# A depthwise convolution of 31 taps: its fourth channel block made by GpSimd in a chain of its own

## The chip, the core and the metric

The kernel runs on one core of a Trainium2 chip. The metric is the device time of one execution in microseconds; the kernel before has a median of 2791.62 us over three runs (2791.62 to 2791.8 us).

## What is computed

Two transformer blocks run one after the other on 256 tokens of width 1024 (and on 256 context tokens in the first layer). The part that matters here is the mixer of the first layer, which joins a gated depthwise convolution with an mLSTM. Its convolution branch, cut to what matters:

```python
def _dwconv(x, w, b):                       # w is 31 taps x 512 channels
    pad = (k - 1) // 2
    y = lax.conv_general_dilated(x, w[:, None, :], (1,), [(pad, k - 1 - pad)], ..., feature_group_count=ch)
    return y + b

def merge(p, h_seq):
    a, g, _, _, _, o, _, _ = p              # projections of the normed input
    u = _dwconv(a * jax.nn.sigmoid(g), conv_w, conv_b)
    u = jax.nn.silu(_layer_norm(u, ln_g, ln_b))
    ...
    return jnp.concatenate([u, hm], axis=-1) @ w_out
```

`merge` is done for the 256 context tokens and the 256 latent tokens, so the convolution works on two segments of 256 tokens, 512 columns in all. All of it is float32.

## The kernel before

Channels lie on the 128 partitions, tokens along the free axis. The 512 channels of the convolution are four blocks of 128. `u0[:, b]` is the gated input of block b with 15 zeros on either side of each segment, `u[:, b]` its output, 128 x 512. The weights of the whole network come from memory as a stream of 1 MB slots through a ring of three slots. SyncE loads a slot into the ring as soon as `slot_read` says that the slot three before it has been used.

The mixer, `mixer0`, has two stretches.

**The projections** (about 60 to 184 us of the span). TensorE works through 20 units of weights, each as three products of a leading and a remaining part. ScalarE cuts the leading part of a unit (`Cut.lead`, line 255), VectorE subtracts it to get the rest (`Cut.rest`, line 264), and there are two buffers, so unit g is cut when unit g-2 has been multiplied. Two units share a slot, and the rest of the odd unit frees it. After each even unit from the third on, TensorE does two products of a second stream, the modulation weights (`later_product`, line 396). After the two units of block b VectorE multiplies value and gate into `u0[:, b]` (line 875) and signals `conv_in_ready`.

**The scans** (184 to 274 us). Eight steps i, four heads by two directions. In each, TensorE makes three modulation products, a row (line 690), waits for `m_weights_ready` and `m_h_taken`, and multiplies decay weights by values (line 713); every second step it also makes the scores (line 680). VectorE adds the mask (line 937), multiplies decays by scores (line 950), and normalizes the result (lines 964 to 977).

The convolution fills VectorE's time in both. `taps(n)` issues the next n taps, each one `scalar_tensor_tensor` of 128 x 512 (line 866; the first tap of a block is line 862), always for the block that has the fewest so far; between two taps of the same block it waits for the earlier. The calls are placed by hand: 4 after each `Cut.rest` while the blocks are made (24 taps), 6 or 3 after each later `Cut.rest` (45), 6 at the end of the projections, and `each` at two places of each scan step, which is the number that is left, 49, divided over 13 places and rounded up: 4. When all is done VectorE signals `conv_done` (line 980), and TensorE takes the mean over the channels with all four blocks of `u` (line 722), which it can't start before step 7 is done.

GpSimd in this stage does four memsets (lines 835 to 838) and then nothing until 1129 us. Its instruction order is its own; it waits only on semaphores.

Of the kernel before, what the change touches and what calls it, by code (L numbers as in the profile page):

```python
# [25 lines left out]
T = 256  # L26
TT = T // P
NTOK = 2 * T
CONV, TAPS = 512, 31
PAD = (TAPS - 1) // 2  # L30
HEADS_M, QK_M, V_M = 4, 64, 128
# [74 lines left out]
def program(nc, stream, table, x_in, out, upto=None):  # L106
    ctx_sems = {}

    def sem(name):

        if name not in ctx_sems:
            ctx_sems[name] = nc.alloc_semaphore(name)
        return ctx_sems[name]
# [3 lines left out]
    h = nc.alloc_sbuf_tensor("h", [P, KD, NTOK], F32)  # L117
# [12 lines left out]
    def col(name):  # L130
        a, n = COL[name]
        if a >= NRES:
            return arena[:, ARENA - NTAB + a:ARENA - NTAB + a + n]
        return tab[:, a:a + n]
# [11 lines left out]
    table_ready, x_ready = sem("table_ready"), sem("x_ready")  # L146
# [436 lines left out]
    def mixer0():  # L583
# [4 lines left out]
        u0 = u0.rearrange("p (b s t) -> p b s t", b=4, s=2)  # L588
        u = u.rearrange("p (b t) -> p b t", b=4)
# [11 lines left out]
        small = nc.alloc_sbuf_tensor("m_small", [P, 64], F32)  # L601
# [12 lines left out]
        def tensor(pe):  # L614
            eng = pe.eng
# [102 lines left out]

            eng.wait_ge(sem("m_h_taken"), 2 * HEADS_M)
            eng.wait_ge(sem("conv_done"), 1)  # L720
            for b in range(4):
                mm = nc.tensor.matmul(ps[:, 7, :], col("over512"), u[:, b, :], start=(b == 0), stop=(b == 3))
            mm.then_inc(N["mean"], 1)
# [108 lines left out]
        def gpsimd(pool):  # L832
# [4 lines left out]
            nc.gpsimd.memset(v1[:, :, :, V_M:V_M + 1], 1.0)  # L837
            nc.gpsimd.memset(zero, 0.0).then_inc(sem("m_borders_ready"), 1)

        def vector(dve):  # L840
            eng = dve.eng
            for k in range(KD):
# [5 lines left out]
            eng.wait_ge(sem("m_borders_ready"), 1)  # L848
            eng.wait_ge(sem("table_ready"), 16)
            cw = col("conv_w").rearrange("p (b t) -> p b t", b=4)  # L850
            last, made = [0] * 4, [0] * 4

            def taps(n, ready=4):

                for _ in range(min(n, 4 * TAPS - sum(made))):
                    b = min(range(ready), key=lambda b: made[b])
                    t = made[b]
                    made[b] += 1
                    o = u[:, b, :].rearrange("p (s t) -> p s t", s=2)
                    i = u0[:, b, :, t:t + T]  # L860
                    if t == 0:
                        last[b] = dve.add(nc.vector.tensor_scalar(o, i, cw[:, b, 0:1], col("conv_b")[:, b:b + 1],
                                                                  ALU.mult, ALU.add))
                    else:
                        dve.settle(last[b])
                        last[b] = dve.add(nc.vector.scalar_tensor_tensor(o, i, cw[:, b, t:t + 1], o,
                                                                         ALU.mult, ALU.add))

            for b in range(4):
                for c in range(2):  # L870
                    C.rest(dve, 2 * b + C.buffers + c)
                    if b:
                        taps(4, b)
                eng.wait_ge(sem("conv_gate_ready"), b + 1)
                nc.vector.tensor_tensor(u0[:, b, :, PAD:PAD + T],
                                        ps[:, 2 * (b % 2), :].rearrange("p (s t) -> p s t", s=2),
                                        sg[:, b, :].rearrange("p (s t) -> p s t", s=2), ALU.mult)\
                  .then_inc(sem("conv_in_ready"), 1)
                eng.wait_ge(sem("conv_in_ready"), b + 1)
# [44 lines left out]
            for g in range(8 + C.buffers, 20):  # L924
                C.rest(dve, g)
                piece = pieces.pop(0) if pieces else None
                if piece:
                    piece()
                taps(3 if piece else 6)
            taps(6)  # L930
            each = -(-(4 * TAPS - sum(made)) // (4 * HEADS_M - 3))

            def diagonal(i):

# [7 lines left out]
            for i in range(2 * HEADS_M):  # L942
# [5 lines left out]
                for j in range(4):  # L948
                    for a, b in spans[d][j]:
                        ins = nc.vector.tensor_tensor(dec[:, j, a * P:b * P], dec[:, j, a * P:b * P],  # L950
                                                      ps[:, j, a * P:b * P], ALU.mult)
# [9 lines left out]
                o = ps[:, 5:7, :].rearrange("p a (b c) -> p (a b) c", b=2)  # L961
# [15 lines left out]
                    nc.vector.tensor_tensor(hs[:, :, hd, :], hs[:, :, hd, :], tmp4[:, :, hd, :], ALU.add)\  # L977
                      .then_inc(sem("m_head_ready"), 1)
            dve.settle()
            nc.vector.tensor_copy(small[:, 60:61], u[:, 3, 0:1]).then_inc(sem("conv_done"), 1)  # L980
            eng.wait_ge(sem("mods0_ready"), 2)
            eng.wait_ge(sem("mods1_ready"), 2)
            eng.wait_ge(sem("m_rms_ready"), 1)
# [20 lines left out]
            for hd in range(HEADS_M):  # L1004
                cuts["ab_out"].input_rest(dve, hd, h[:, hd, :])

        return dict(name=name, tensor=tensor, scalar=scalar, vector=vector, gpsimd=gpsimd)


# [1766 lines left out]

    add(start(), ada_first(norms["mix0_mod"]["pe"], norms["mix0_mod"]["act"], norm0.pop("vector")))
    add(norm0, mixer0())
    add(out_proj("mix0_out", "ab_out", 0, mixer0_ready, 0, 2, then="ffn0_mod", nxt="ffn0_up"))
    add(modulate("ffn0_mod", 0, 0, 3, done("mix0_out", "x"), 6, "ffn0_up", held=17))  # L2780
# [18 lines left out]
    if upto is not None:  # L2799
        n = [s["name"] for s in stages].index(upto[0])  # L2800
# [263 lines left out]
```

## Time and profile before

| | us |
|---|---|
| median of three runs | 2791.62 |
| span of the profiled execution | 2782.0 |
| TensorE busy | 2667.0 |
| VectorE busy | 1925.3 |
| ScalarE busy | 1517.7 |
| GpSimd busy | 18.1 |

The profiled execution has no time of its own beside its span. The span runs from its first to its last instruction, and the median of the runs is 9.6 us longer; a difference within the span is taken as a difference of the run. Busy times are those of one engine over the whole span, and the engines overlap. TensorE (PE) is busy nearly throughout, so what matters is where it stands idle. The chip grants it one of two clocks, shown as a share of 2.4 GHz. Times below are microseconds from the start of the span unless marked ns.

### The profile page before, as it was taken

What the parts mean: (1) busy time and instruction counts of PE and PEld (TensorE: products, weight loads), DVE (VectorE), ACT (ScalarE), POOL (GpSimd) and SP (SyncE); (2) the same over time, 40 slices, a digit from 0 to 9 for tenths busy, and PEclk for the clock granted to TensorE, in tenths of its full rate; (3) what the DMA queues carried; (4) which work ended last, traced back from release to release, by engine and by line L of the source; (5) the groups of instructions that cost most, each with busy time, mean ns of one, the idle gap of its engine ahead of it and who ended that gap; (6) DMA issues with size and microseconds to landing.
All of it is one profiled execution on the core that took longest, in us unless ns stands there. A gap on an engine that the chain in (4) does not pass through costs nothing.

```text
span 2782.0 us, 39479 instructions
## 1 busy us (share of the span) xinstructions
PE 2667.0 (96%) x14416; PEld 2189.5 (79%) x14416; DVE 1925.3 (69%) x2538; ACT 1517.7 (55%) x2202; POOL 18.1 (1%) x20
## 2 busy tenths in 40 slices
PE   7998999999998999989999999999999999999997
PEld 3764778888655899869999867888888888888886
DVE  2676655543267676575555655789898988989896
ACT  3233442322355544355444354678787877878784
POOL 0000000000000000000001000000000000000000
PEclk9998999999999999999999989999999999999999
DMA  6656122222220445324553312599999989989893
GB/s 257 242 225 274 61 91 93 104 91 91 91 76 31 147 172 182 122 76 147 185 184 137 121 61 106 199 350 379 346 370 352 367 350 350 364 343 376 348 364 136
DMA packets 80644, 581.53 MB, mean 209 GB/s; under 512 B 8848, under 2 KB 10128, under 8 KB 10128
## 3 DMA queue, kind: packets, MB, share of 16 engines
q1 hardware_dynamic: 80528, 579.90, 55.4%
q8 instruction: 82, 1.34, 0.2%
q14 instruction: 34, 0.28, 0.0%
HBM read 578.82 MB, written 1.05 MB: 208 GB/s over the span
## 4 chain that ended last, share of the span: by engine, by line
PE 85%; DVE 8%; ACT 3%; DMA 2%; issue 1%; POOL 0%; SPq 0%; ACTq 0%; DVEq 0%
PE ps L2482 7%; PE ps L2484 7%; PE ps L2483 7%; PE ps L289 7%; PE ps L290 7%; PE ps L291 7%; PE ps L2509 4%; PE ps L2511 4%; PE ps L2510 4%; PE ps L1114 3%; PE ps L1112 3%; PE ps L1113 3%; DVE parts L264 2%; DMA ring<-in_stream_dram 2%; PE ps L396 1%; PE ps L308 1%
## 5 line engine op out<-in xcount | busy, mean ns | idle before, releaser
L264 DVE TENSOR_TENSOR parts<-ring,parts 128x1024 fp32r<-128x1024 f32 x294 | 357.4, 1224 | 407.0 <-ACT parts L255 394.8
L255 ACT ACTIVATE parts<-ring 128x1024 fp32r<-128x1024 f32 x294 | 307.7, 1054 | 456.7 <-PE ps L291 196.2
L289 PE MATMUL ps<-parts 128*128 128x256 f32 (+1 forms) x1472 | 474.9, 323 | 8.6 <-DVE arena L1184 5.4
L290 PE MATMUL ps<-parts 128*128 128x256 f32 (+1 forms) x1472 | 470.0, 319 | 0.0
L291 PE MATMUL ps<-parts 128*128 128x256 f32 (+1 forms) x1472 | 469.6, 319 | 0.0
L2707 DVE TENSOR_TENSOR parts<-ring,parts 128x1024 fp32r<-128x1024 f32 x280 | 331.8, 1218 | 12.0 <-ACT parts L2549 0.3
L2549 ACT ACTIVATE parts<-ring 128x1024 fp32r<-128x1024 f32 x280 | 291.9, 1060 | 55.7 <-PE ps L2484 47.3
L289 PEld LDWEIGHTS ps<-parts 128*128 128x128 f32 x1472 | 280.5, 191 | 38.4 <-DVE arena L1184 9.4
L2482 PE MATMUL ps<-parts 128*128 128x512 f32 x752 | 296.8, 395 | 0.5 <-DVE parts L2707 0.5
L290 PEld LDWEIGHTS ps<-parts 128*128 128x128 f32 x1472 | 280.6, 191 | 19.8 <-issue 0.2
L291 PEld LDWEIGHTS ps<-parts 128*128 128x128 f32 x1472 | 280.7, 191 | 19.6
L2484 PE MATMUL ps<-parts 128*128 128x512 f32 x752 | 293.2, 390 | 0.0
L2483 PE MATMUL ps<-parts 128*128 128x512 f32 x752 | 292.8, 389 | 0.0
L2707 DVE TENSOR_TENSOR parts<-h,parts 128x1024 fp32r<-128x1024 f32 x224 | 264.4, 1218 | 7.9
L2549 ACT ACTIVATE parts<-h 128x1024 fp32r<-128x1024 f32 x224 | 234.1, 1062 | 44.1 <-PE ps L2484 34.7
L1112 PE MATMUL ps<-arena_r,parts 128*128 128x256 f32 (+1 forms) x576 | 182.1, 316 | 0.0
L1114 PE MATMUL ps<-arena_r,parts 128*128 128x256 f32 (+1 forms) x576 | 182.1, 316 | 0.0
L2484 PEld LDWEIGHTS ps<-parts 128*128 128x128 f32 x752 | 141.1, 188 | 30.1
L2482 PEld LDWEIGHTS ps<-parts 128*128 128x128 f32 x752 | 141.3, 188 | 29.3 <-DVE parts L2707 1.6
L2483 PEld LDWEIGHTS ps<-parts 128*128 128x128 f32 x752 | 141.3, 188 | 27.8
L1113 PE MATMUL ps<-arena_r,parts 128*128 128x256 f32 (+1 forms) x520 | 160.0, 308 | 0.0
L2509 PE MATMUL ps<-parts,arena_r 128*128 128x512 f32 x368 | 144.4, 392 | 0.0
(414 smaller groups left out, 4745.3 us busy)
## 6 DMA issues: line engine op xcount, KB each, us to landing
ring<-in_stream_dram SPq DMA_DIRECT2D x380, 1024.0 KB, 5.7
h<-in_stream_dram SPq DMA_DIRECT2D x112, 1024.0 KB, 7.1
arena<-in_stream_dram SPq DMA_DIRECT2D x56, 1024.0 KB, 7.1
x<-in_x_dram SPq DMA_DIRECT2D x1, 2048.0 KB, 7.8
tab<-in_table_dram SPq DMA_DIRECT2D x1, 1724.5 KB, 10.1
out_dram<-x SPq DMA_DIRECT2D x1, 1024.0 KB, 4.8
tab<-in_table_dram SPq DMA_DIRECT2D x1, 184.5 KB, 2.7
arena<-in_table_dram SPq DMA_DIRECT2D x1, 144.0 KB, 13.6
```

Source lines behind the costliest of these rows:

```text
L255: nc.scalar.activation(self.w_lead[:, self.buffer(g)], units(ring[:, n % NS, :])[:, g % UPS], ACT.Copy)\
L264: nc.vector.tensor_tensor(self.w_rest[:, self.buffer(g)], units(ring[:, n % NS, :])[:, g % UPS], self.w_lead[:, self.buffer(g)].bitcast(F3 ...
L289: nc.tensor.matmul(dst, wl[:, k, :], xl, start=(k == 0), stop=False)
L290: nc.tensor.matmul(dst, wl[:, k, :], xr, start=False, stop=False)
L291: mm = nc.tensor.matmul(dst, wr[:, k, :], xl, start=False, stop=(k == KD - 1))
L1112: nc.tensor.matmul(dst, a, hid_lead[f], start=(f == 0), stop=False)
L1114: mm = nc.tensor.matmul(dst, b, hid_lead[f], start=False, stop=(f == nblk - 1))
L2482: nc.tensor.matmul(dst, x_lead[:, k, :], wl[:, m, :], start=(k == 0), stop=False)
L2483: nc.tensor.matmul(dst, x_lead[:, k, :], wr[:, m, :], start=False, stop=False)
L2484: mm = nc.tensor.matmul(dst, x_rest[:, k, :], wl[:, m, :], start=False, stop=(k == KD - 1))
L2549: nc.scalar.activation(w_lead[i % CUTS], buffers[b][:, (i % 2) * UNIT:(i % 2 + 1) * UNIT], ACT.Copy).then_inc(S("lead"), 1)
L2707: nc.vector.tensor_tensor(w_rest[i % CUTS], buffers[i // 2 % RING][:, (i % 2) * UNIT:(i % 2 + 1) * UNIT], w_lead[i % CUTS].bitcast(F32), A ...
```

## The change

VectorE makes the taps of blocks 0 to 2 only, 93 instead of 124. `taps` gets its default `ready=3`, and its calls stay where they are; the number left for the scans becomes 18, so that `each` is 2 instead of 4. The fourth block, `u[:, 3]`, is made by GpSimd. It waits until `u0` is complete (`conv_in_ready` at 4), makes the first tap with one `tensor_scalar`, and each of the other 30 taps with a multiplication by the tap's weight into one of two scratch halves of `h[:, 6:8]` and an addition onto `o`: 61 instructions in all. Before each addition `settle` waits until all that GpSimd has issued before it is complete. TensorE waits for `conv_last_block` beside `conv_done` before the mean. Nothing else uses those two blocks of `h` in that time.

```diff
@@ -718,6 +718,7 @@
 
             eng.wait_ge(sem("m_h_taken"), 2 * HEADS_M)
             eng.wait_ge(sem("conv_done"), 1)
+            eng.wait_ge(sem("conv_last_block"), 1)
             for b in range(4):
                 mm = nc.tensor.matmul(ps[:, 7, :], col("over512"), u[:, b, :], start=(b == 0), stop=(b == 3))
             mm.then_inc(N["mean"], 1)
@@ -837,6 +838,21 @@
             nc.gpsimd.memset(v1[:, :, :, V_M:V_M + 1], 1.0)
             nc.gpsimd.memset(zero, 0.0).then_inc(sem("m_borders_ready"), 1)
 
+            cw = col("conv_w").rearrange("p (b t) -> p b t", b=4)
+            o = u[:, 3, :].rearrange("p (s t) -> p s t", s=2)
+            pool.eng.wait_ge(sem("m_borders_ready"), 1)
+            pool.eng.wait_ge(sem("table_ready"), 16)
+            pool.eng.wait_ge(sem("conv_in_ready"), 4)
+            product = h[:, 6:8, :].rearrange("p n (s t) -> p n s t", s=2)
+            pool.add(nc.gpsimd.tensor_scalar(o, u0[:, 3, :, 0:T], cw[:, 3, 0:1], col("conv_b")[:, 3:4], ALU.mult, ALU.add))
+            for t in range(1, TAPS):
+                pool.add(nc.gpsimd.tensor_scalar(product[:, t % 2], u0[:, 3, :, t:t + T], cw[:, 3, t:t + 1], None, ALU.mult))
+                pool.settle()
+                ins = nc.gpsimd.tensor_tensor(o, o, product[:, t % 2], ALU.add)
+                if t < TAPS - 1:
+                    pool.add(ins)
+            ins.then_inc(sem("conv_last_block"), 1)
+
         def vector(dve):
             eng = dve.eng
             for k in range(KD):
@@ -848,11 +864,11 @@
             eng.wait_ge(sem("m_borders_ready"), 1)
             eng.wait_ge(sem("table_ready"), 16)
             cw = col("conv_w").rearrange("p (b t) -> p b t", b=4)
-            last, made = [0] * 4, [0] * 4
-
-            def taps(n, ready=4):
-
-                for _ in range(min(n, 4 * TAPS - sum(made))):
+            last, made = [0] * 3, [0] * 3
+
+            def taps(n, ready=3):
+
+                for _ in range(min(n, 3 * TAPS - sum(made))):
                     b = min(range(ready), key=lambda b: made[b])
                     t = made[b]
                     made[b] += 1
@@ -928,7 +944,7 @@
                     piece()
                 taps(3 if piece else 6)
             taps(6)
-            each = -(-(4 * TAPS - sum(made)) // (4 * HEADS_M - 3))
+            each = -(-(3 * TAPS - sum(made)) // (4 * HEADS_M - 3))
 
             def diagonal(i):
 
@@ -977,7 +993,7 @@
                     nc.vector.tensor_tensor(hs[:, :, hd, :], hs[:, :, hd, :], tmp4[:, :, hd, :], ALU.add)\
                       .then_inc(sem("m_head_ready"), 1)
             dve.settle()
-            nc.vector.tensor_copy(small[:, 60:61], u[:, 3, 0:1]).then_inc(sem("conv_done"), 1)
+            nc.vector.tensor_copy(small[:, 60:61], u[:, 2, 0:1]).then_inc(sem("conv_done"), 1)
             eng.wait_ge(sem("mods0_ready"), 2)
             eng.wait_ge(sem("mods1_ready"), 2)
             eng.wait_ge(sem("m_rms_ready"), 1)
```

## Rows read from the trace of the kernel before

**Rows 1.** The page, part 1: busy time, share of span, instructions.
```profile
...
PE 2667.0 (96%) x14416; PEld 2189.5 (79%) x14416; DVE 1925.3 (69%) x2538; ACT 1517.7 (55%) x2202; POOL 18.1 (1%) x20
...
```

**Rows 2.** Windows: span, busy of PE, PEld, DVE, ACT, POOL, clock, DMA.
```profile
...
111.00:184.00 73.00, 71.11 (x339) 51.84 (x332) 57.17 (x78) 19.14 (x26) 0.00 (x0) 0.98 0.58 220
184.00:274.50 90.50, 73.77 (x427) 40.64 (x425) 65.34 (x147) 30.43 (x95) 0.00 (x0) 0.89 0.71 279
...
```

**Rows 3.** Chain of waits from 182 us: start, duration, what.
```profile
...
192.65 7.88 DMA ring<-in_stream_dram
...
201.85 9.47 DMA ring<-in_stream_dram
...
219.71 2.73 DVE arena L866 x4
222.44 1.67 DVE parts_f L950 x5
...
224.15 4.00 PE ps L713 x20
...
233.84 8.10 DMA ring<-in_stream_dram
...
```

**Rows 4.** TensorE's waits, 184 to 275 us: total, times, longest.
```profile
...
PE ps L396 <- DMA ring<-in_stream_dram: 9.8, 7, 2.7
...
PE ps L713 <- DVE parts_f L950: 2.4, 1, 2.4
...
```

**Rows 5.** Timeline of TensorE: start, duration, line, form, [idle before].
```profile
...
217.89 2.78 PE L396 MATMUL ps<-ring,silu_c 128*32 128x512 f32 x24
220.60 1.12 PE L690 MATMUL ps<-arena,tab 4*128 4x512 f32 x2
224.15 4.00 PE L713 MATMUL ps<-arena,parts_f 128*128 128x129 f32 x20 [2.43 <-DVE parts_f L950]
...
234.70 2.50 PE L713 MATMUL ps<-arena 128*128 128x129 f32 x20
...
274.54 5.37 PE L722 MATMUL ps<-arena,tab 128*128 128x512 f32 x8 [2.77 <-DVE m_small L980]
...
```

**Rows 6.** VectorE's groups, 111 to 176.1 us: busy, mean, idle before.
```profile
...
L866 DVE SCALAR_TENSOR_TENSOR arena<-arena,tab 128x512 f32<-128x512 f32 x39 | 27.1, 746 | 0.4
L264 DVE TENSOR_TENSOR parts<-ring,parts 128x1024 fp32r<-128x1024 f32 x10 | 12.2, 1224 | 15.1 <-ACT parts L255 15.1
L905 DVE TENSOR_TENSOR arena<-arena 4x512 f32<-4x512 f32 x2 | 1.4, 678 | 0.0
...
L910 DVE TENSOR_TENSOR_SCAN arena<-arena 4x256 f32<-4x256 f32 x1 | 0.7, 681 | 0.0
...
L885 DVE TENSOR_SCALAR arena<-arena 128x512 f32<-128x512 f32 x1 | 0.4, 420 | 0.0
...
```

**Rows 7.** Timeline of ScalarE in the same stretch.
```profile
...
125.51 1.06 ACT L255 ACTIVATE parts<-ring 128x1024 fp32r<-128x1024 f32 x1 [5.44 <-DMA ring<-in_stream_dram]
...
179.20 0.60 ACT L774 ACTIVATE arena<-ps 128x512 f32<-128x512 f32 x1 [3.35 <-PE ps L291]
...
```

**Rows 8.** Timeline of VectorE, 110 to 185 us, columns as in rows 5.
```profile
...
110.30 0.69 DVE L875 TENSOR_TENSOR arena<-ps,arena 128x512 f32<-128x512 f32 x1
...
174.91 1.23 DVE L264 TENSOR_TENSOR parts<-ring,parts 128x1024 fp32r<-128x1024 f32 x1 [2.36 <-ACT parts L255]
176.05 8.03 DVE L866 SCALAR_TENSOR_TENSOR arena<-arena,tab 128x512 f32<-128x512 f32 x12
...
```

**Rows 9.** Windows of 4 us around that wait, columns as in rows 2.
```profile
...
220.00:224.00 4.00, 1.72 (x10) 0.29 (x2) 4.00 (x9) 0.00 (x0) 0.00 (x0) 0.99 0.92 346
224.00:228.00 4.00, 3.85 (x20) 3.81 (x20) 3.34 (x6) 2.36 (x7) 0.00 (x0) 0.59 1.01 426
...
```

**Rows 10.** Timeline of GpSimd, whole span.
```profile
...
53.85 0.53 POOL L838 MEMSET arena<- 128x512 f32 x1
...
1576.53 0.95 POOL L2183 MEMSET parts_f<- 128x1024 f32 x1
...
```

## The prediction

> **What bounds the kernel now.** I read the page first. TensorE is busy for 96% of the span and GpSimd for 18.1 us of it, so GpSimd is free and VectorE is not the bound of the kernel as a whole [rows 1]. Then the windows of the two stretches in which the change acts. From 111 to 184 us TensorE is busy for 71.11 of 73 us and VectorE for 57.17. From 184 to 274.5 us TensorE is busy for 73.77 of 90.5, so there are 16.7 us to be had at most [rows 2].
>
> Next the chain of waits and TensorE's waits in the second stretch. The chain goes mostly through TensorE and transfers of weights: 7.88, 9.47, 8.10 us from the issue of a slot to its landing [rows 3]. Of TensorE's idle time 9.8 us end with a slot's landing and only 2.4 us with VectorE, once, before line 713 of step 3 [rows 4]. That is the only place before 274 us at which a tap stands on the chain: four taps (2.73 us) and then line 950 (1.67 us), for which line 713 waits [rows 3, 5].
>
> In the first stretch VectorE must be in time with its line 264. It is, but it has little to spare. It stands idle for 15.1 us there, always before line 264 and always for ScalarE's line 255 [rows 6]. ScalarE in turn waits for a slot before the even units (5.44 us at 125.51) [rows 7], and that slot could only be loaded once VectorE had freed one.
>
> **The change part by part.**
>
> *Taps taken from VectorE.* 31 of 124 instructions go. Twelve taps in a row take 8.03 us, 0.67 each [rows 8], so 31 are 20.8 us. But the calls in the projections are fixed numbers (24, then 45, then 6), and they find enough taps in three blocks. VectorE issues as many taps up to 184 us as before. All 31 are taken from the scans, where 18 are left instead of 49.
>
> *What that is worth.* The 18 taps are used up at two a place by the first place of step 4. At step 3's first place two taps stand ahead of line 950 instead of four, half of the 2.73 us: line 713 of step 3 can start 1.37 us earlier. It can't gain more from the taps lost at the place before, since VectorE's work on step 2's result begins when TensorE has made it, and those taps turn into idle time. TensorE's own order allows 2.43 us, as row 690 ends at 221.7 [rows 5], so the 1.37 us come through, and TensorE still waits 1.06 us. One thing more: after this wait the granted clock is 0.59 in the mean, so part of the window is at 1.2 GHz, and line 713 takes 4.00 us where it takes 2.50 us a step later [rows 5, 9]. If the shorter wait kept the clock up, 1.5 us would be added, 2.9 us in all. I take 1.4 us, since a wait remains. The other taps taken away stood beside waits for slots and save nothing: VectorE becomes idle instead.
>
> *GpSimd's chain.* It can start when line 875 of the fourth block is done, 111.0 us [rows 8]. GpSimd reads SBUF nowhere in the trace before; the nearest rows are its memsets, 0.53 us for 512 columns and 0.95 us for 1024, which makes 0.43 us for a pass over 512 columns and 0.10 us beside it [rows 10]. A multiplication reads once and writes once. It takes 0.53 us if the two overlap and 0.95 us if they don't. An addition reads two tensors and writes one: 0.53, 0.95 or 1.38 us for one, two or three passes. For the multiplication I take 0.53 us, since it has one pass each way and is nearest to the memset, and for the addition 0.95 us, two reads through one interface with the write beneath. The sum is 31 x 0.53 + 30 x 0.95 = 44.9 us. The bounds are 61 x 0.53 = 32.3 us and 31 x 0.95 + 30 x 1.38 = 70.9 us. Waits between instructions come on top for the chain's end, though not for what it holds. Even the upper bound ends at 111 + 70.9 = 182 us if nothing holds it; TensorE asks for the block at 274 us [rows 5], where it now waits for VectorE's last step. So the chain by itself is hidden, and the added wait costs nothing.
>
> The Trainium skill ("GPSIMD Engine Reference", section 3.1) gives 4497 ns for an addition of 2048 float32 columns and 769 ns for a light loop over 512. An estimate from that page is 1.12 us for an addition and 0.77 us for a multiplication, 57.5 us in all, and the sum below would end at 2829.5 us by it. No run here shows either.
>
> *What the chain holds up.* This is the term that decides. In 111 to 176.1 us VectorE has 49 taps and rests (39 and 10), 39.3 us, and 11 smaller instructions of the gates with two inputs in SBUF (the first and last group of these are shown, ten groups), 9.3 us [rows 6]. So 60 of its instructions read two tensors of SBUF while GpSimd has 61 that read SBUF as well. A second input is not free for VectorE even alone: at the same 512 columns line 905 takes 678 ns and line 885, with one input, 420 [rows 6]. No row shows the two engines reading at once, so the cost of that lies between nothing and the whole of GpSimd's time. At the upper end the two take turns: each GpSimd instruction holds back one VectorE instruction for its own length, and there are as many of the one as of the other.
>
> What VectorE can absorb is known from rows. Its idle time is 15.1 us [rows 6]. Its last rest (line 264 at 174.91, 1.23 us) ends at 176.1 [rows 8], and TensorE has finished unit 18, whose result ScalarE reads at 179.20, only 3.1 us later [rows 7]; unit 19 needs that rest. Together that is 18.2 us. Slots cost nothing on top while VectorE is behind, since it has taps to do while one lands.
>
> With turns taken, TensorE is late at unit 19 by 44.9 - 18.2 = 26.7 us. What remains of VectorE's order after that is shorter than before. The delay goes through to the end, because nothing after 184 us has time to give but the waits for slots, and the ring is full at that point in both kernels.
>
> The Trainium skill ("SBUF — State Buffer", section "Who interferes with whom") says that a VectorE instruction with two SBUF inputs contends with a GpSimd instruction that reads SBUF, and that the later of the two is blocked until the other is through. No row here shows it. By that rule the sum is the one just made.
>
> **The sum.** 26.7 - 1.4 = +25.3 us on the span, so 2791.6 + 25.3 = 2817 us. With the bounds it is 32.3 - 18.2 - 2.9 = +11 us (2803) to 70.9 - 18.2 = +53 us (2844). About 0.2% (5.6 us) is what a measurement of this kernel can tell from no change. It takes 18.2 + 1.4 + 5.6 = 25.2 us of holding up to be slower by that much: 0.41 us for each of the 61 instructions, less than the shortest memset of that width.
>
> **The rivals.**
>
> *VectorE isn't held up, or by no more than it can absorb.* This is the case on the other side. The two inputs may be read without harm to each other, or it may be GpSimd that is held: VectorE issues taps back to back, and GpSimd then gets the idle time and what is left after 184 us, where most of VectorE's inputs are in PSUM. Its chain has 274.5 - 111 - 44.9 = 118 us to spare. The place is step 3's wait, and the price -1.4 to -2.9 us: 2788.7 to 2790.2 us, no change that can be told. It decides when the holding is under 18.2 us in all, 0.30 us an instruction. For it speaks that no row shows harm; against it that the stretch has 60 exposed instructions and 15 us of air.
>
> *More is freed than I count.* An earlier step 3 could also bring the transfers of steps 4 to 7 forward and keep the clock up there. The 9.8 us of waits for slots are the most that could be added, and it needs over 5.6 us to be seen: about 2784 us. Against it: a slot lands 8 to 9 us after its issue, whatever VectorE does [rows 3].
>
> *GpSimd's chain is late itself.* If a tap of it takes over (274.5 - 111) / 31 = 5.3 us, with its waits and holdings, TensorE stands at the mean. At 6 us a tap it ends at 297, 22.5 us late: 2813 us. Nothing in the rows is near it: a memset is a tenth of that.
>
> **How the numbers follow.** The forecast (VectorE held up by more than its air) has 0.66, VectorE not held 0.24, more freed 0.06, the chain late 0.04. Forecast and late chain are slower, 0.70; not held is the same, 0.24; more freed is faster, 0.06. The likeliest case alone has the range 2803 to 2844. With the second case the range is 2788 to 2844, which leaves out less than 2 in 10.
>
> **What would show it.** In the trace after, line 866 and line 264 between 111 us and GpSimd's last addition should be longer than 746 and 1224 ns, or stand idle between, by one GpSimd instruction each at most, and should be as before once GpSimd is through. VectorE's idle time before line 264 should be gone, TensorE should wait for line 264 from about 125 us on, and the scans should start some 27 us later. GpSimd's multiplications should be near 0.53 us and its additions near 0.95. The wait of line 722 should still be for VectorE's last step. In step 3 line 713's wait for line 950 should be 1.4 us shorter. The prediction is wrong if line 866 keeps its 746 ns beside a working GpSimd, or if GpSimd's own instructions are the ones that grow; and it is too high if the two engines share the reads rather than take turns.

## The result and the profile after

The kernel after takes 2802.10 us, the kernel before 2790.79 us (medians of twelve runs each). The ratio is 1.004 with a 95% interval of 1.0028 to 1.0051, so 8 to 14 us slower. The sign was right. The size was not: 25 us were forecast and 11 measured. The time lies inside the full range of 2788 to 2844 us and just under the 2803 at which the likeliest case began.

Single executions of either kernel spread over 14 us and more (2779.86 to 2795.68 before), so a difference between two profiles isn't yet one between kernels. In both kernels a run's time is about 1.8 us over its span. My reading that the median lies 9.6 us over the span was wrong: the profile before is of one of the quickest executions (2782.0 + 1.8 = 2783.8 us).

To compare executions I use two lengths throughout. The *projections* run from the start of the last line 875 (110.3 us before; line 891 after) to the start of ScalarE's last sigmoid (184.6 before, 198.4 after). The *scans* run from there to `conv_done` (274.3 before, 292.4 after). The first length has two values where nothing is held. It is 74.3 us or so where the granted clock is 0.97 in the mean up to the last rest, as in the profile before, and 72.7 us where it is 1.00 and line 875 starts some 2 us later. The last sigmoid starts at 184.4 to 186.0 us in all of these. The profile after, whose line 891 starts at 112.6, is of the later kind, so that its loss lies between 11.5 us by length (85.8 against 74.3) and 14 us by the sigmoid's start.

The page after, parts 1 and 2 (the line that answers to [rows 1], and GpSimd's busy tenths):

```profile
## 1 busy us (share of the span) xinstructions
PE 2677.6 (96%) x14416; PEld 2191.1 (78%) x14416; DVE 1941.1 (69%) x2507; ACT 1517.5 (54%) x2202; POOL 127.0 (5%) x81
...
POOL 0392000000000000000000100000000000000000
```

VectorE has 31 instructions fewer and is busy for 15.8 us longer. Its groups between line 891 and its last rest, 113.3 to 192.4 us after, against [rows 6]:

```profile
L882 DVE SCALAR_TENSOR_TENSOR arena<-arena,tab 128x512 f32<-128x512 f32 x40 | 46.2, 1213 | 0.2
L264 DVE TENSOR_TENSOR parts<-ring,parts 128x1024 fp32r<-128x1024 f32 x10 | 14.3, 1431 | 2.5 <-ACT parts L255 2.5
...
L901 DVE TENSOR_SCALAR arena<-arena 128x512 f32<-128x512 f32 x1 | 0.4, 416 | 0.0
```

Forty taps take 46.2 us where 39 took 27.1. The idle time before the rests has gone from 15.1 to 2.5 us, and line 901, with one input, keeps its 0.42 us; it ran beside a multiplication. Not every instruction with one input does (see the last section). TensorE's waits from 111 to 200 us, which had none for line 264 before, and GpSimd's groups in 113.3 to 192.4 us:

```profile
PE ps L396 <- DVE parts L264: 6.3, 3, 3.2
PE ps L289 <- DVE parts L264: 2.3, 1, 2.3
...
PE ps L654 <- DVE parts L264: 0.5, 1, 0.5
```

```profile
L849 POOL TENSOR_SCALAR h<-arena,tab 128x512 f32<-128x512 f32 x21 | 48.6, 2316 | 0.0
L851 POOL TENSOR_TENSOR arena<-arena,h 128x512 f32<-128x512 f32 x20 | 29.7, 1486 | 1.7
```

The turns can be seen in the timelines after. GpSimd first, then VectorE:

```profile
182.79 3.07 POOL L849 TENSOR_SCALAR h<-arena,tab 128x512 f32<-128x512 f32 x1
185.94 1.40 POOL L851 TENSOR_TENSOR arena<-arena,h 128x512 f32<-128x512 f32 x1
187.33 2.00 POOL L849 TENSOR_SCALAR h<-arena,tab 128x512 f32<-128x512 f32 x1
```

```profile
186.11 1.78 DVE L882 SCALAR_TENSOR_TENSOR arena<-arena,tab 128x512 f32<-128x512 f32 x1
```

```profile
187.82 1.18 DVE L882 SCALAR_TENSOR_TENSOR arena<-arena,tab 128x512 f32<-128x512 f32 x1
```

The addition starts at 185.94, the tap at 186.11, and the tap ends at 187.89, 0.55 us after the addition's end: it stood still for the addition, and took 1.78 us instead of 0.75. The next tap meets a multiplication and takes 1.18 us, 0.43 longer, though the multiplication goes on until 189.33. The multiplication in turn took 3.07 and 2.00 us; with VectorE idle, or on an instruction with one input in SBUF, it takes 1.56, as in the scans, where the next one starts 2.9 us later, at 221.75:

```profile
218.86 1.56 POOL L849 TENSOR_SCALAR h<-arena,tab 128x512 f32<-128x512 f32 x1
220.51 1.26 POOL L851 TENSOR_TENSOR arena<-arena,h 128x512 f32<-128x512 f32 x1
```

VectorE's last rest, against [rows 8]:

```profile
191.26 1.21 DVE L264 TENSOR_TENSOR parts<-ring,parts 128x1024 fp32r<-128x1024 f32 x1
192.40 13.77 DVE L882 SCALAR_TENSOR_TENSOR arena<-arena,tab 128x512 f32<-128x512 f32 x12
```

Twelve taps took 8.03 us and now take 13.77. From the end of line 891 (113.3) the last rest ends after 79.2 us; before, it was 176.1 - 111.0 = 65.1. It is 14.1 us later, TensorE had 3.1 us to spare, and the projections are 85.8 us long instead of 74.3: 11.5 us. GpSimd's chain ends at 224.9, 67 us before the mean needs it.

### The profile page after: what moved, and what is told of

Read it like the earlier page. It is cut to its first block, busy times and chain, and to the rows that moved or that the text cites. A ratio compares the mean times of both kernels' runs of the same rounds, so it can differ in the third digit from the quotient of the medians.

```text
span 2800.2 us, 39512 instructions
## 1 busy us (share of the span) xinstructions
PE 2677.6 (96%) x14416; PEld 2191.1 (78%) x14416; DVE 1941.1 (69%) x2507; ACT 1517.5 (54%) x2202; POOL 127.0 (5%) x81
## 4 chain that ended last, share of the span: by engine, by line
PE 83%; DVE 11%; ACT 3%; DMA 2%; issue 1%; SPq 0%; ACTq 0%; DVEq 0%
PE ps L2498 7%; PE ps L2500 7%; PE ps L2499 7%; PE ps L289 6%; PE ps L291 6%; PE ps L290 6%; PE ps L2525 4%; PE ps L2527 4%; PE ps L2526 4%; PE ps L1130 3%; PE ps L1128 3%; PE ps L1129 3%; DVE parts L264 3%; DMA ring<-in_stream_dram 2%; DVE arena L882 2%; PE ps L308 1%
```

## The experiments

All ratios are to the kernel before on the same chip.

**e1: VectorE's part alone.** The chain is cut after its first instruction; the convolution's fourth block lacks 30 taps.

```diff
-            pool.add(nc.gpsimd.tensor_scalar(o, u0[:, 3, :, 0:T], ...))
-            for t in range(1, TAPS):
-                ...
-            ins.then_inc(sem("conv_last_block"), 1)
+            nc.gpsimd.tensor_scalar(o, u0[:, 3, :, 0:T], ...).then_inc(sem("conv_last_block"), 1)
```

> VectorE makes blocks 0 to 2 only, as in the kernel after, but GpSimd makes only the first tap of the fourth block; its other 30 taps are left out. Theory (the loss is GpSimd and VectorE taking turns at reading SBUF in the projections): without the chain no VectorE instruction is held, line 882 is back at 0.67 us from start to start, the last rest ends about 65 us after line 891 of the fourth block as before, and the time is before less 1.4 to 2.9 us. Rival (the loss lies in VectorE's own order, three blocks in turn instead of four, or in the shorter scans): the time stays 5 us or more above before with no chain beside it.

Measured: ratio 0.9973 (0.9959 to 0.9987), 2779.83 us. Projections 72.7 us, scans 90.2. Nothing in VectorE's own order costs time; all of the loss needs the chain. The gain is 4 to 11 us, more than the 1.4 to 2.9 that both the prediction and this expectation gave. e9 comes back to it.

**e2: the chain beside all of VectorE's work.** The kernel before with GpSimd's code added, and `conv_last_block` waited for.

```diff
+            o = h[:, 2, :].rearrange("p (s t) -> p s t", s=2)      # scratch; u[:, 3] stays VectorE's
+            ... (GpSimd's 61 instructions as in the change)
```

> The kernel before, whole, with GpSimd's 61 instructions added: the same reads, but the sums go to a scratch block of h and are used for nothing; VectorE makes all 124 taps. Theory: the projections are late by the same 11 us as in the kernel after, and the scans, which have four taps a place again, lose some more while the chain runs: before plus 14 to 20 us. Rival (the loss comes from what was taken from VectorE, not from what was given to GpSimd): no more than 2 us from before.

Measured: ratio 1.0064 (1.0043 to 1.0085), 12 to 24 us slower. Projections 89.7 us, scans 98.8. The total came as expected. The rival falls: the loss comes with what GpSimd was given. The chain alone costs the projections 15 us here, more than the expected 11; a second profile of the kernel after (a1 below) has 89.5 us as well.

**e3: sixteen taps, in the scans.** VectorE makes 108 taps, GpSimd the last 16 of the fourth block after the projections.

```diff
+        CAPS, reached = (TAPS, TAPS, TAPS, 15), [0]
+            pool.eng.wait_ge(sem("m_gcol_ready"), 1)
+            pool.eng.wait_ge(sem("vector_steps"), reached[0])       # VectorE's 15th tap of block 3
+            for t in range(CAPS[3], TAPS):
```

> GpSimd makes only the last 16 taps of the fourth block, starting when the scans start (its chain waits for the gate columns and for VectorE's first 15 taps of that block); VectorE makes 108 taps, of which 75 lie before the scans as before, and 33 in them, three a place. Theory: in the projections nothing is held, so that they take as long as before; in the scans VectorE has time to give, and each held tap costs nothing but at step 3: before less 0 to 2 us. Rival (GpSimd's reads cost wherever they lie, at some 0.37 us for each of its instructions, as 11 us over 31 taps would make it per tap): before plus 5 us or more.

Measured: ratio 1.0015 (1.0001 to 1.0029), +4 us. Projections 74.3 us, exactly as before: with GpSimd silent nothing is held there. But the scans don't take it for nothing, as I had expected. TensorE's wait before line 714 (713 before):

```profile
PE ps L714 <- DVE parts_f L968: 3.9, 1, 3.9
```

It was 2.4 us [rows 4], and with two shorter ones the waits for line 968 come to 5.0 us. The theory (less 0 to 2 us) is out. The rival's 5 us or more lies within the interval, 0.3 to 8 us, so its time isn't excluded. The scans took 93.9 us, which the kernel before takes too (b1 and b2 below). The place matters for the projections, but the first steps of the scans have little air either.

**e4: fewer taps beside the rests.** The kernel after with one edit.

```diff
-                taps(3 if piece else 6)
+                taps(1 if piece else 3)
```

> The kernel after, with the same chain on GpSimd, but VectorE makes only 1 or 3 taps behind each rest of the later projections instead of 3 or 6: 20 taps there instead of 45, and 43 left for the scans, four a place. Theory: 25 taps are 17 us of VectorE's time, and with the 18 us that it can absorb they cover what GpSimd holds before the last rest, about 29 us; the projections end in time, TensorE doesn't wait for line 264, the scans start at full clock: before plus 0 to 3 us. Rival (GpSimd costs TensorE's time by another way than VectorE's lateness, for instance by the transfers or the clock): the 11 us stay.

Measured: ratio 1.0010 (0.9997 to 1.0022), and the projections are back at 74.3 us, with no wait of TensorE for line 264 left. Of GpSimd's 61 instructions 36 ran before the last rest, against 42 in the kernel after. So the loss of the projections is VectorE's lateness at line 264, and the rival falls. The scans take 96.4 us and now show waits, 3.1 + 2.4 + 2.1 = 7.6 us:

```profile
PE ps L403 <- DVE parts_f L966: 3.1, 1, 3.1
...
PE ps L713 <- DVE parts_f L966: 2.4, 1, 2.4
PE ps L403 <- DVE arena L966: 2.1, 2, 1.7
```

**m5, m6, m7: which instruction holds how much.** In each, the kernel before is whole and GpSimd works on scratch from 111 us on: 30 multiplications, 30 additions, or 92 memsets of 1024 columns.

```diff
+            for t in range(1, TAPS):                    # m5
+                pool.add(nc.gpsimd.tensor_scalar(product[:, t % 2], u0[:, 3, :, t:t + T], ...)); pool.settle()
+            for t in range(1, TAPS):                    # m6
+                pool.settle(); pool.add(nc.gpsimd.tensor_tensor(o, o, product[:, t % 2], ALU.add))
+            for t in range(1, 3 * TAPS):                # m7
+                pool.add(nc.gpsimd.memset(h[:, 6:8, :], 0.0)); pool.settle()
```

> The kernel before, whole, with GpSimd doing the 30 multiplications alone into scratch blocks of h (each waits for the one before), and no additions. Theory (a GpSimd instruction that reads SBUF holds VectorE's instructions with two SBUF inputs, a multiplication for one pass of reading, about 0.4 us, although it takes 2 us itself): all 30 fall in the projections and hold 12 us, less than the 18.2 us that VectorE absorbs; TensorE waits little for line 264, and the time is before plus 0 to 3 us. Rival (each GpSimd instruction holds VectorE for all of its own length): 30 x 1.6 to 2.0 is 48 to 60 us held, and TensorE is 30 us or more late.

> The kernel before, whole, with GpSimd doing the 30 additions alone on scratch blocks of h, each waiting for the one before, and no multiplications. Theory: an addition holds VectorE for all of its own reading, about 1.05 us; they come twice as densely as in the kernel after, 1.3 to 1.9 us apart, so that they all lie between 111 and about 165 us, hold 30 x 1.05 = 31 us against some 12 us of idle time there and 3 us to spare, and TensorE is late by 13 to 17 us: before plus 12 to 18 us. Rival (multiplication and addition hold alike, 0.7 us each): 21 us held, before plus 4 to 8 us.

> The kernel before, whole, with GpSimd writing zeros to scratch blocks of h from the same moment on: 92 memsets of 1024 columns in a chain, 0.95 us each, so some 95 us of them, and no reads. Theory (it is the reading of SBUF that the two engines share): line 866 and line 264 keep 746 and 1224 ns, VectorE's idle time stays 15 us, and the time is that of before within 2 us. Rival (any work of GpSimd on SBUF holds VectorE): 60 instructions of VectorE are held and the time is 10 us or more above before.

Measured: m5 1.0008 (0.9994 to 1.0021), m6 1.0070 (1.0047 to 1.0092), m7 0.9995 (0.9977 to 1.0013). The times of m5 and m7 came as expected, and m6's 13 to 26 us are at and above the expected 12 to 18. The projections took 76.8, 95.7 and 74.4 us. m5's are 2.5 us longer than before, though I had expected all that it holds to be absorbed:

```profile
PE ps L396 <- DVE parts L264: 2.1, 2, 1.1
```

Timelines of m5, VectorE and GpSimd:

```profile
165.98 5.28 DVE L879 SCALAR_TENSOR_TENSOR arena<-arena,tab 128x512 f32<-128x512 f32 x6
```

```profile
153.34 17.60 POOL L848 TENSOR_SCALAR h<-arena,tab 128x512 f32<-128x512 f32 x9
```

Six taps take 5.28 us instead of 6 x 0.67 = 4.0, while a multiplication comes every 17.60 / 9 = 1.96 us: 1.3 us for 2.7 of them, 0.47 us each. The same of m6:

```profile
118.70 8.45 DVE L882 SCALAR_TENSOR_TENSOR arena<-arena,tab 128x512 f32<-128x512 f32 x5
```

```profile
116.23 12.04 POOL L851 TENSOR_TENSOR h<-h 128x512 f32<-128x512 f32 x7
```

Each tap takes 1.69 us and each addition 1.72: turns, one for one, 1.0 us held by each. m7's VectorE groups from 111 to 176.1 us:

```profile
L880 DVE SCALAR_TENSOR_TENSOR arena<-arena,tab 128x512 f32<-128x512 f32 x38 | 26.4, 747 | 0.4
L264 DVE TENSOR_TENSOR parts<-ring,parts 128x1024 fp32r<-128x1024 f32 x10 | 12.2, 1223 | 11.9 <-ACT parts L255 11.9
L932 DVE TENSOR_SCALAR arena<-arena 4x512 f32<-4x512 f32 x2 | 2.3, 1146 | 0.0
```

With 63 memsets beside them the two-input instructions keep their lengths. It is GpSimd's reads that hold them. VectorE's idle time, which I had expected to stay at 15 us, is 11.9; the last section comes to that. Three rivals fall: that each instruction holds for all its own length (m5), that the two kinds hold alike (m6), and that any work of GpSimd does (m7).

**e8 and e9: taps later in the scans.** e8 is e4 with the edit below; e9 is the kernel before with it and nothing on GpSimd.

```diff
-            each = -(-(3 * TAPS - sum(made)) // (4 * HEADS_M - 3))
+            def each(i):
+                return 2 if i < 4 else 4 if i < 7 else 3 * TAPS      # e9: 4 * TAPS
-                taps(each)
+                taps(each(i))
```

> As e4_taps_moved (whole chain on GpSimd, 1 or 3 taps behind each rest), but the 43 taps of the scans are placed later: two at each place of steps 0 to 3, four at each place of steps 4 to 6, the rest in step 7. In e4 TensorE waited 7.6 us for line 966 in the scans, with four taps a place and GpSimd still reading. Theory: with half the taps ahead of line 966 while GpSimd reads, most of that wait goes: less than 2 us of TensorE's waits end with line 966, and the time is 2 to 5 us under e4, so before less 0 to 3 us. Rival (the scans are set by slots and the clock alone): the waits for slots grow by what the waits for line 966 lose, and the time is that of e4 within 1 us.

> The kernel before with nothing on GpSimd; the 49 taps of the scans are placed later in the same way, two at each place of steps 0 to 3, four in steps 4 to 6, nine in step 7 where VectorE stood idle for 11 us. Theory (what e1 gained of 7 us came from fewer taps ahead of line 950 in the first steps, not from VectorE's total): the 2.4 us wait in step 3 goes, and the time is before less 1 to 7 us, the same as e1 within its interval, and under every kernel with a chain on GpSimd. Rival (the total of VectorE's taps matters, not their place): the time is that of before within 1 us.

Measured: e8 0.9974 (0.9962 to 0.9986), e9 0.9982 (0.9971 to 0.9994). Both beat both kernels: e8 is 4 to 11 us under the kernel before and e9 2 to 8. For e8 that is more than the 0 to 3 us expected. For e9 it is as expected, except that it isn't under e8. In e8, TensorE's waits from 184 to 282 us:

```profile
PE ps L396 <- DMA ring<-in_stream_dram: 10.6, 7, 2.9
...
PE ps L713 <- DVE parts_f L967: 0.3, 1, 0.3
```

The 7.6 us of e4 are 0.3, and the waits for slots have grown from 8.1 to 10.6 only. In e9 the wait in step 3 is gone, but the nine taps of step 7 brought another:

```profile
PE ps L403 <- DVE parts_f L951: 2.1, 1, 2.1
```

So e9 is quicker although TensorE waits for VectorE almost as long as before, 2.1 us instead of 2.4. Projections 72.7 us in both, scans 89.7 (e8) and 90.6 (e9). e1, e8 and e9 have two things in common, two taps a place in steps 0 to 3 and a gain of 5 to 7.5 us by the ratio, whether VectorE makes 93 taps or 124 and whether or not GpSimd works. So it was the place of the taps that gave e9 its gain, and it can account for e1's; by which waits or clock it comes isn't shown. GpSimd's chain is worth nothing measurable: e8 and e9 can't be told apart.

**b1, b2, a1: the same kernels again.** The first profiles had scans of 89.7 us before and 94.0 after, which would be 4.3 us of loss outside the projections.

> The kernel before, unchanged, profiled once more. In the first pair of profiles the scans took 89.7 us before and 94.0 us after, and 96.0 us in a kernel whose VectorE and TensorE did the same as before (m7). Theory: the projections are the same within 0.5 us in every execution (74.3 us from line 875 of the fourth block to the last sigmoid), but the scans vary by some 5 us from one execution to the next with the granted clock, so that this look gives 90 to 96 us. Rival: the scans of the kernel before repeat within 1 us at 89.7, and the 4.3 us more after the change belong to it.

> The same once more, for a third look. Theory: scans between 90 and 96 us and not the same as in the look before; projections 74.3 us. Rival: 89.7 us again.

> The kernel after, unchanged, profiled once more. Theory: the projections take 85.8 us again, 11.5 more than before, since instruction lengths and the order of the turns set them; the scans fall between 90 and 96 us as they do before. Rival: the scans take 94 us again while those of the kernel before repeat at 89.7.

Measured (one execution each, 2788.68, 2795.83 and 2805.54 us): scans 94.8 and 100.0 us in the kernel before, 94.1 in the kernel after. Projections 74.4 and 72.7 before, 89.5 after. The 4.3 us can't be put down to the change: the scans of the kernel before range over 10 us, twice what I had expected. The projections repeat within 2 us before, not within 0.5; those of the kernel after came 3.7 us longer in this profile than in the first, more than I had expected. TensorE's wait for line 950, 2.4 us in the first profile, was 0.9 and 1.1 us in b1 and b2. The chip's clock has a part in the scans' range. TensorE's timeline at their start, in b1:

```profile
187.09 1.09 PE L690 MATMUL ps<-arena,tab 4*128 4x512 f32 x2 [0.83 <-ACT arena L776]
188.12 5.06 PE L680 MATMUL ps<-arena 64*128 64x512 f32 x8
193.10 3.90 PE L396 MATMUL ps<-ring,silu_c 128*32 128x512 f32 x24
```

In the first profile before the same eight and twenty-four matmuls took 2.84 and 2.78 us, with the same 0.83 us of idle time ahead of them. The mean granted clock of the scans was 0.89 there, 0.84 in b1 and 0.79 in b2, whose scans were the longest.

## Why the prediction was right in sign and wrong in size

*What bounds the kernel* held. The chain of the fourth block ends 67 us before it is needed, and the wait at line 722 is still for VectorE's last step.

*That the two engines take turns* held for additions, down to single instructions: a tap that meets an addition ends 0.55 us after it. GpSimd's own instructions grew as well. The prediction called it a sign of being wrong if they grew in place of VectorE's; here both grow: a multiplication from 1.56 us to 2.32 in the mean ahead of the last rest, an addition from 1.26 to 1.49. The Trainium skill ("SBUF — State Buffer", section "Who interferes with whom") says that a VectorE instruction with two SBUF inputs contends with a GpSimd instruction that reads SBUF and not with one that only writes; m6 (1.0 us held by each addition) and m7 (747 ns beside memsets, 746 without) agree. Its "exclusive lock", which the prediction took to last until the other is through, doesn't fit the multiplication: that one takes 1.56 to 3.07 us and holds 0.47.

*What VectorE can absorb* was near for this change, 15.2 us instead of 18.2. VectorE used 12.6 of the 15.1 us of idle time, and of the 3.1 us to spare 2.6 show (the last rest came 14.1 us later and the projections grew by 11.5). But it isn't a fixed stock, as the sum had it. In m5 VectorE was busy for 8.3 us more than before, far less than 18.2, and yet the projections were 2.5 us longer, with 5.8 us of idle time used. In m6 it was busy for 28.2 us more, the projections were 21.4 us longer, and 5.8 us of waits for line 255 came after GpSimd's last addition at 167.0 us, too late to be of use. TensorE waits at earlier rests too (2.1 us in m5, 15.2 in m6), so idle time can absorb only what was held before it and hasn't yet reached TensorE.

*What one pair of GpSimd instructions holds* was near: 0.53 + 0.95 = 1.48 us forecast, 0.47 + 1.0 = 1.47 by m5 and m6. In the kernel after, four pairs beside the last twelve taps hold (13.77 - 8.03) / 4 = 1.44 us each. For the multiplication that is luck. The 0.53 us was meant as its whole length, which is 1.56 us or more, and it holds for a third of that or less; the two errors cancel.

*The step that failed* is that GpSimd's instructions hold for their own length, and with it the count: "there are as many of the one as of the other", so that all 61 GpSimd instructions would fall ahead of the last rest. I took what its instructions hold for their length and so for GpSimd's pace, and said that waits between them count only for the chain's end. But the pace sets how many of them fall in the stretch that matters. A multiplication takes 1.56 us alone and mostly 2.0 to 3.1 beside taps, an addition 1.26 and up to 2.3, so that a tap of GpSimd takes 2.9 us alone and (224.9 - 113.5) / 31 = 3.6 us on average, not 1.5. Ahead of the last rest were 22 instructions with one tensor and 20 additions. They should hold 22 x 0.47 + 20 x 1.0 = 30.3 us. Between the end of line 891 (875 before) and that of the last rest VectorE was not waiting for line 255 for 79.2 - 2.5 = 76.7 us, where it had been 65.1 - 15.1 = 50.0, so 26.7 were held; the rest may have met idle time or work that isn't held. The term of 44.9 us was 26.7, and 26.7 - 15.2 gives the 11.5 us by which the projections grew in this profile. The remaining third of the chain ran in the scans.

*The gain of 1.4 us in step 3* is a second term that was mis-sized: by the medians e1 gains 4 to 11 us and e9 2 to 8, with fewer taps ahead of line 950. So the change's 11 us aren't the projections' loss alone, though the two numbers are alike. The chain without the relief (e2) costs 18 us and the relief without the chain (e1) gains 7.5, and 18 - 7.5 = 10.5 us is what the change shows within its interval. The forecast had 26.7 - 1.4.

Where the gain comes from stays open. In the kernel after only 0.4 us of waits for line 966 (950 before) is left, but the 2.4 us from which I priced the gain were 0.9 and 1.1 in b1 and b2, and e9 has its gain with waits of 2.1 us. One profile of each can't show where it lies, since the scans of the kernel before took 89.7, 94.8 and 100.0 us. Those of e1, e8 and e9 took 90.2, 89.7 and 90.6. Whether fewer waits keep the clock up, or the transfers come out better, stays open.

*The rivals.* "VectorE isn't held up, or by no more than it can absorb" is out by m6 and e2; "the chain is late" never came near. "More is freed" is true of e1 and hidden in the change under the larger loss. One reading of the prediction was off without harm: the ten groups that it adds up to 9.3 us make 8.6.

## What to carry to other kernels

Work moved from VectorE to GpSimd isn't free when VectorE is busy with two-input instructions: a multiplication and an addition of 512 columns that both met such work took 1.47 us of VectorE's time, and the tap that it saved was worth 0.67. For the price, count how many GpSimd instructions fall before the point that TensorE waits for, and for that count take GpSimd's whole pace, not what it holds. And before moving work to another engine, try moving it in time: e9 gained 2 to 8 us with nothing on GpSimd, by two taps instead of four at each place of the first steps.

## What the runs showed of the hardware that was not expected

It is not only the reads that collide. With memsets on GpSimd (m7) one-input VectorE instructions from SBUF to SBUF grew now and then: line 932 (918 before) takes 1146 ns in the mean where it took 413, line 899 (885 before) takes 1.25 us instead of 0.42, and VectorE's idle time falls by 3.2 us. Two-input instructions did not grow. Beside additions those with one input grew as well: in the kernel after line 907, a copy, takes 1405 ns where it took 422, and in m6 line 901 takes 1.49 us and the copies of lines 906 and 907 take 1.38 and 1.40. Beside a multiplication it was 0.42 us once (line 901 in the kernel after) and 0.84 once (the same instruction, line 898, in m5).

A GpSimd multiplication of 512 float32 columns by one weight per partition takes 1.56 us alone, three times a memset of the same size (0.53), and longer than an addition of two tensors (1.26). It can't be priced from the memset. The chain's first instruction, a multiplication and addition of a constant in one, is recorded with 0.76 us; why it is so much shorter isn't shown.
